# A decoder layer on one core: a wide stream in the first feed-forward product, GpSimd's squares moved into it, and a reordered opening

## What is computed

```
u = rms_norm(h, norm_mix);  z = u @ w_in                      # 1024 x 3328
h = h + concat(rwkv7_time_mix(z[:1792]), moba_attention(z[1792:])) @ w_mix_out
h = h + memory_cross_attention(rms_norm(h, norm_xattn), rms_norm(mem, norm_mem))   # w_xq, w_xkv, w_xo
a = square(relu(rms_norm(h, norm_ffn) @ w_ff1))               # 1024 x 4096
h = h + a @ w_ff2                                             # 4096 x 1024
out = rms_norm(h, norm_final)
```

## Time and profile before

| | us |
|---|---|
| median of 3 runs | 477.54 |
| lowest, highest | 476.89, 479.78 |
| the profiled execution | 479.23 |
| its span, first to last instruction | 477.2 |
| TensorE busy | 459.2 |
| VectorE busy | 316.0 |
| ScalarE busy | 235.7 |
| GpSimd busy | 34.8 |
| mean granted clock of TensorE | 0.994 |

### The profile page before, as it was taken

The page is one execution under the profiler, slowest core; times in us unless marked ns, Lnnn a source line. Parts: engine busy times, 40 slices in busy tenths (PEclk is TensorE's granted clock), DMA queues, the critical chain, the costliest instruction groups (busy, mean ns, idle before and its releaser), DMA issues.

```text
span 477.2 us, 11032 instructions
## 1 busy us (share of the span) xinstructions
PE 459.2 (96%) x4774; PEld 429.8 (90%) x4774; DVE 316.0 (66%) x459; ACT 235.7 (49%) x357; POOL 34.8 (7%) x50
## 2 busy tenths in 40 slices
PE   4999999999999999999999997999999999999994
PEld 4999999989898899999998997989898989898983
DVE  4688999897576459668656486555466555554646
ACT  5779843343354235335543453544374555453534
POOL 8100000000000000151000053000000000000000
PEclk9999999999999999999999998999999999999998
DMA  7963534505060523554452363756555555756602
GB/s 256 332 218 102 177 105 159 182 10 172 3 203 15 166 89 99 168 177 142 133 166 89 94 181 97 232 169 198 178 178 177 177 181 178 233 195 205 197 2 88
DMA packets 61411, 73.09 MB, mean 153 GB/s; under 512 B 1314, under 2 KB 51572, under 8 KB 61364
## 3 DMA queue, kind: packets, MB, share of 16 engines
q1 hardware_dynamic: 61284, 72.14, 47.3%
q0 software_dynamic: 80, 0.26, 0.1%
HBM read 71.35 MB, written 1.05 MB: 152 GB/s over the span
## 4 chain that ended last, share of the span: by engine, by line
PE 90%; DVE 5%; issue 1%; DMA 1%; ACT 1%; SPq 0%; ACTq 0%; DVEq 0%
PE bank L482 17%; PE bank L483 16%; PE bank L484 16%; PE bank L499 6%; PE bank L500 6%; PE bank L501 6%; PE bank L449 2%; PE bank L450 2%; PE bank L451 2%; PE bank L851 2%; DMA xval<-in_x 1%; PE bank L875 1%; PE bank L611 1%; DVE w_lo L1543 1%; PE bank L777 1%
## 5 line engine op out<-in xcount | busy, mean ns | idle before, releaser
L1543 DVE TENSOR_TENSOR w_lo<-raw,w_hi 128x1024 fp32r<-128x1024 f32 x130 | 160.3, 1242 | 84.2 <-ACT w_hi L1051 84.0
L1051 ACT ACTIVATE w_hi<-raw 128x1024 fp32r<-128x1024 f32 x130 | 136.6, 1057 | 140.0 <-PE bank L484 80.1
L482 PE MATMUL bank<-op_hi,w_hi 128*128 128x256 f32 x672 | 195.1, 290 | 3.8 <-DVE w_lo L1543 3.0
L483 PE MATMUL bank<-op_lo,w_hi 128*128 128x256 f32 x672 | 190.7, 284 | 0.4 <-issue 0.4
L484 PE MATMUL bank<-op_hi,w_lo 128*128 128x256 f32 x672 | 190.7, 284 | 0.0
L482 PEld LDWEIGHTS bank<-op_hi,w_hi 128*128 128x128 f32 x672 | 129.4, 192 | 6.7 <-issue 4.6
L483 PEld LDWEIGHTS bank<-op_lo,w_hi 128*128 128x128 f32 x672 | 129.5, 193 | 0.5
L484 PEld LDWEIGHTS bank<-op_hi,w_lo 128*128 128x128 f32 x672 | 129.4, 193 | 0.4 <-issue 0.4
L499 PE MATMUL bank<-w_hi,op_hi 128*128 128x512 f32 x128 | 49.9, 390 | 0.0
L500 PE MATMUL bank<-w_lo,op_hi 128*128 128x512 f32 x128 | 49.9, 390 | 0.0
L501 PE MATMUL bank<-w_hi,op_lo 128*128 128x512 f32 x128 | 49.8, 389 | 0.0
(11 more groups left out here) (247 smaller groups left out, 487.1 us busy)
## 6 DMA issues: line engine op xcount, KB each, us to landing
raw<-in_w_ff SPq DMA_DIRECT2D x32, 1024.0 KB, 5.4
raw<-in_w_in SPq DMA_DIRECT2D x12, 1024.0 KB, 5.5
raw<-in_w_xkv SPq DMA_DIRECT2D x8, 1024.0 KB, 5.7
raw<-in_w_mix_out SPq DMA_DIRECT2D x4, 1024.0 KB, 5.0
raw<-in_w_xq SPq DMA_DIRECT2D x4, 1024.0 KB, 5.1
raw<-in_w_xo SPq DMA_DIRECT2D x4, 1024.0 KB, 5.7
xval<-in_x SPq DMA_DIRECT2D x2, 512.0 KB, 4.8
raw<-in_w_in SPq DMA_DIRECT2D x2, 512.0 KB, 5.7
```

Of the source, the lines that this page charges most:

```text
L482: mm(dst, wh[:, k, :], op_hi[which][:, k, :], start=first, stop=False)
L483: mm(dst, wh[:, k, :], op_lo[which][:, k, :], start=False, stop=False)
L1051: op(view(w_hi), r, ACT.Copy).then_inc(hi_done, 1)
L1543: tt(view(w_lo), r, view(w_hi).bitcast(f32), ALU.subtract).then_inc(lo_done, 1)
```

## The change

- **Wide stream.** In `f1`, `op_hi[0]` and `op_lo[0]` become one tile `op_both[0]`, and for each k one matmul of 2 x 256 columns multiplies `w_hi` with both; one of 256 adds `w_lo` times `op_hi` to the left half of the bank. Each half has a bank of its own, in turn, and its result is the sum of the bank's two sides. ScalarE copies the right side out (`part`), VectorE adds the left (`add`) and does Relu and square in one (`square`), ScalarE rounds it to `op_hi[1]`, VectorE subtracts.
- **First f1 unit.** Its quarters run (66,0), (67,0), (66,1), (67,1), no longer with half 68 between.
- **GpSimd's squares** of `xo` wait besides for the ends of halves 67, 70, 73, 76; `rms(3)` moves from behind 27 quarters to behind 46.
- **Opening.** x comes in quarters; `norm_mix` is sent by ScalarE; unit 1 is sent ahead of the parameters; 14 identity products (`warm`) stand around the turns of x; VectorE's `copies(0)` moves behind `lo(3)`; some steps of the first six outputs are put in another order, `sums()` ahead of `take(3)` among them.

```diff
-    _late = {"mix": 0, "xo": 1, "f1": 1}.get(UNITS[_u][0])
+    _late = {"mix": 0, "xo": 1}.get(UNITS[_u][0])
...
-    elif _u == len(UNITS) - 1:
+    elif _u == len(UNITS) - 1 or UNITS[_u][0] == "f1" and UNITS[_u][4] == 0:
 
         QUARTERS += [(2 * _u + _i, _p) for _p in range(2) for _i in range(2)]
...
+        op_both = [sb("op0", [128, 2, KT, T], f32r), None]
+        op_hi = [op_both[0][:, 0, :, :], sb("op1_hi", [128, KT, T], f32r)]
+        op_lo = [op_both[0][:, 1, :, :], sb("op1_lo", [128, KT, T], f32r)]
...
+        def half_no(s):
+            return s - OUTS[FIRST["f1"]][1] if UNITS[s // 2][4] < 2 else 2 * UNITS[s // 2][4] + s % 2
+        def half_bank(s):
+            return dense_bank[(s + 1) % 2]
...
-            sp.dma_start(prow[0:8, :], io["norm_mix"].rearrange("l (r p) -> (l r) p", p=128)).then_inc(mix_in, 16)
...
             for half in range(2):
-                c, k = slice(512 * half, 512 * half + 512), slice(4 * half, 4 * half + 4)
-                sp.dma_start(stage[0][:, :, c], x[:, :, c]).then_inc(x_in[half], 16)
+                for q in (2 * half, 2 * half + 1):
+                    c = slice(256 * q, 256 * q + 256)
+                    sp.dma_start(stage[0][:, :, c], x[:, :, c]).then_inc(x_in[q], 16)
+                k = slice(4 * half, 4 * half + 4)
...
+            load_unit(1)
             for name, (r, c) in ROW.items():
...
-            load_unit(1)
...
                     pool.wait_ge(out_taken, FIRST[what] + j + 1)
+                    if count:
+                        pool.wait_ge(dense_mm, OUTS[FIRST["f1"]][1] + 2 + 3 * j)
...
+                    if what == "f1":
+                        half = half_no(s)
+                        if half < 2:
+                            pe.wait_ge(out_taken, FIRST["f1"] - 1 + half)
+                        else:
+                            pe.wait_ge(dve_add, half - 1)
...
+                if what == "f1":
+                    b = half_bank(s)
+                    for k in range(4 * part, 4 * part + 4):
+                        first, final = q == BEGUN[s] and k % 4 == 0, q == DONE[s] and k % 4 == 3
+                        if opening and k % 2 == 0:
+                            pe.wait_ge(dve_op, op_no("xo", k // 2) + 1)
+                        if final:
+                            mm(b[:, 0:T], wl[:, k, :], op_hi[0][:, k, :], start=False, stop=False)
+                        last = mm(b[:, :], wh[:, k, :], op_both[0][:, :, k, :], start=first, stop=final)
+                        if not final:
+                            mm(b[:, 0:T], wl[:, k, :], op_hi[0][:, k, :], start=False, stop=False)
...
+            def warm(n):
+                for _ in range(n):
+                    turn_op(dense_bank[1][:, 0:128], ident[:, :], ident[:, :])
...
             params(0)
+            warm(4)
             load(0, 0)
             load(0, 1)
+            warm(7)
             load(0, 2)
             load(0, 3)
+            warm(3)
+            dense(3)
+            params(1)
+            dense(1)
+            spread(0)
+            dense(9)
+            lora()
...
-            dense(27)
+            dense(46)
             rms(3)
-            dense(28)
+            dense(9)
             residual(0)
...
+            def part(n, half):
+                s = OUTS[FIRST["f1"] + n][1] + half
+                act.wait_ge(dense_mm, s + 1)
+                if n >= 2:
+                    act.wait_ge(dve_square, n - 1)
+                op(tmp[:, n % 2, T * half:T * half + T], half_bank(s)[:, T:2 * T], ACT.Copy).then_inc(act_part, 1)
             def hidden(o):
                 n = nth(o)
-                act.wait_ge(out_taken, o + 1)
+                act.wait_ge(dve_square, n + 1)
                 k = 4 * (n // 2 % 2) + 2 * (n % 2)
-                op(op_hi[1][:, k:k + 2, :], pair(tmp[:, n % 2, :]), ACT.Square).then_inc(act_hidden, 1)
+                op(op_hi[1][:, k:k + 2, :], pair(hid_sq[:, n % 2, :]), ACT.Copy).then_inc(act_hidden, 1)
...
+            def add(n, half):
+                s = OUTS[FIRST["f1"] + n][1] + half
+                dve.wait_ge(act_part, 2 * n + half + 1)
+                x = tmp[:, n % 2, T * half:T * half + T]
+                tt(x, half_bank(s)[:, 0:T], x, ALU.add).then_inc(dve_add, 1)
+            def square(n):
+                dve.wait_ge(dve_add, 2 * n + 2)
+                if n >= 2:
+                    dve.wait_ge(dve_hidden, n - 1)
+                x = tmp[:, n % 2, :]
+                stt(out=hid_sq[:, n % 2, :], in0=x, scalar=0.0, in1=x, op0=ALU.max, op1=ALU.mult).then_inc(dve_square, 1)
...
             params(0)
             load(0, 0)
-            copies(0)
+            lo(0)
             load(0, 1)
-            lo(0)
...
             spread_copy(0)
+            copies(0)
+            copies(1)
+            take(0)
             lo(4)
...
+            add(4, 0)
             lo(81)
+            add(4, 1)
+            square(4)
             lo(82)
+            hidden(4)
...
```

More of the change, by code:

```diff
@@ L1442, in _ @@
             hi(80)
+            part(4, 0)
             hi(81)
-            take(36)
+            part(4, 1)
             hi(82)
-            follow(36)
+            follow(37)
+            part(5, 0)
             hi(83)
+            part(5, 1)
             hi(84)
+            follow(38)
             hi(85)
-            take(37)
             hi(86)
@@ L1456, in _ @@
             hi(89)
-            follow(37)
-            take(38)
-            follow(38)
-            take(39)
+            part(6, 1)
+            hi(90)
             follow(39)
-            hi(90)
+            part(7, 0)
             hi(91)
-            take(40)
+            part(7, 1)
+            hi(92)
             follow(40)
-            hi(92)
             hi(93)
@@ L2151, in _ @@
             follow(32)
+            add(0, 0)
             lo(69)
-            follow(33)
+            add(0, 1)
+            square(0)
             lo(70)
+            hidden(0)
+            add(1, 0)
             lo(71)
+            add(1, 1)
+            square(1)
             lo(72)
+            hidden(1)
+            add(2, 0)
             lo(73)
+            add(2, 1)
+            square(2)
             lo(74)
-            follow(34)
+            hidden(2)
+            add(3, 0)
             lo(75)
+            add(3, 1)
+            square(3)
             lo(76)
-            follow(35)
+            hidden(3)
             lo(77)
@@ L2166, in _ @@
             lo(80)
+            add(4, 0)
             lo(81)
-            follow(36)
-            rms(3)
+            add(4, 1)
+            square(4)
             lo(82)
+            hidden(4)
+            add(5, 0)
             lo(83)
+            add(5, 1)
+            square(5)
             lo(84)
+            hidden(5)
             lo(85)
@@ L2175, in _ @@
             lo(87)
+            rms(3)
             lo(88)
+            add(6, 0)
             lo(89)
-            follow(37)
-            follow(38)
-            follow(39)
+            add(6, 1)
+            square(6)
             lo(90)
+            hidden(6)
+            add(7, 0)
             lo(91)
-            follow(40)
+            add(7, 1)
+            square(7)
             lo(92)
+            hidden(7)
             lo(93)
@@ L2188, in _ @@
             lo(96)
+            add(8, 0)
             lo(97)
-            follow(41)
+            add(8, 1)
+            square(8)
             lo(98)
+            hidden(8)
+            add(9, 0)
             lo(99)
-            follow(42)
+            add(9, 1)
+            square(9)
             lo(100)
+            hidden(9)
             lo(101)
@@ L2198, in _ @@
             lo(104)
+            add(10, 0)
             lo(105)
-            follow(43)
+            add(10, 1)
+            square(10)
             lo(106)
+            hidden(10)
+            add(11, 0)
             lo(107)
-            follow(44)
+            add(11, 1)
+            square(11)
             lo(108)
+            hidden(11)
             lo(109)
@@ L2208, in _ @@
             lo(112)
+            add(12, 0)
             lo(113)
-            follow(45)
+            add(12, 1)
+            square(12)
             lo(114)
+            hidden(12)
+            add(13, 0)
             lo(115)
-            follow(46)
+            add(13, 1)
+            square(13)
             lo(116)
+            hidden(13)
             lo(117)
@@ L2218, in _ @@
             lo(120)
+            add(14, 0)
             lo(121)
-            follow(47)
+            add(14, 1)
+            square(14)
             lo(122)
+            hidden(14)
+            add(15, 0)
             lo(123)
-            follow(48)
+            add(15, 1)
+            square(15)
             lo(124)
+            hidden(15)
             lo(125)
```

149 lines of the change are left out of this document (75 added, 74 removed).

## The result

| | before | after |
|---|---|---|
| median | 477.7 us (4 runs, 476.89 to 479.78) | 471.95 us (4 runs, 471.72 to 472.79) |
| the profiled execution | 479.23 | 472.15 |
| its span | 477.2 | 470.3 |
| TensorE busy | 459.2 | 457.3 |
| VectorE busy | 316.0 | 323.4 |

The ratio of the times is 0.9866, with a 95% interval of 0.984 to 0.9892: 1.3% faster (1.2% by the medians). The forecast was 469.8 in a range of 467.3 to 473.0. The medians lie 5.75 us apart, the profiled spans 6.9; the forecast had 7.9 and 9.3. So the kind of result is as forecast, and some 2 us of the gain are missing. The time lies in the range, but outside the stretch of 468.3 to 471 to which the forecast gave its 0.50.

The account below looks back on a forecast made before the run. TensorE, with 90% of the chain, was taken to bound the kernel. Seam 3.1, clock 1.5, wide stream 3.4, squares -0.2 and opening 1.5 made 9.3 us, giving 469.9 (469.7 without the dip); forecast 469.8, range 467.3 to 473.0.

Parts of the forecast that it names:

- The seam: Between xo and the first f1 product: TensorE's 3.2 us stall shrinks to some 0.1; gain 3.1 us.
- The clock's dip: Behind the stall at xo to f1: without that pause the granted clock should not fall to 0.50; gain 1.5 us.
- The wide stream: In f1: one 512-column matmul replaces two of 256, 0.360 us per k becomes 0.347; gain 3.4 us.
- The handshake: Rival in f1: late adds make every half wait 0.5 us, 16 us in all, giving 485.8; chance 0.04.
- The squares' new cover: In f1: GpSimd's held-back squares hold up VectorE there; 0.2 us put on the path, 1.5 if nothing overlaps.
- (a): Opening: only four turns and three identity products follow x's last quarter; first product at 9.7, 0.35 us sooner.
- (b): Opening: 14 identity products keep TensorE working nearly throughout, so the clock is up by the first product; worth 1.6 us.
- (c): Opening, a cap: unit 1 needs lo(2), whose chain moves only with x's last quarter; start 16.4, gain 1.5 us.
- (d): Opening: load_unit(1) passes the parameter loads, which come at about 12.5; TensorE asks at 14.0, covered by 1.5 us.
- (e): Opening: copies(0) moves behind lo(3), where VectorE's waits cover it; bare, it would cost 1.3 us.
- (f): Past 39 us: the opening's gain lives only if VectorE's whole string moves too, which it does.
- the opening gives nothing: Rival: VectorE's string from 39 to 84 us stays put and TensorE only waits longer there; 471.3 us, chance 0.14.

Follow-up runs that it names:

- Experiment 3: The changed kernel without GpSimd's wait for the f1 halves, so the xo squares start again as soon as hT is taken; 476.13 us (ratio 0.9954).
- experiment 4: The kernel before with only GpSimd's xo squares held back to the ends of halves 67, 70, 73, 76 and rms(3) moved; 475.4 us (ratio 0.9942).
- experiment 1: The changed kernel with op_hi and op_lo of one k laid out as 512 columns in a row; 472.34 us (ratio 0.9877).
- experiment 2: The changed kernel with the wide matmul taken apart into two of 256 columns; 474.42 us (ratio 0.9931).
- experiment 7: The changed kernel with x in two halves instead of four quarters; 472.04 us (ratio 0.9857).
- experiment 5: The changed kernel with each f1 quarter's four wide matmuls in a row and four narrow ones in a row; 472.55 us (ratio 0.987).
- experiment 8: The changed kernel with the whole opening of the kernel before, keeping the change's seam, squares and wide stream; 471.87 us (ratio 0.9861).

## Why the prediction was right, and where it was not

**The seam: right, 3.2 us for 3.1.** The walk put `follow(31)` at 0.87 and (67,0) at 285.8. The pair took 0.88, and the matmul starts at 285.75. Experiment 3 brings the stalls back by one edit, and experiment 4 shows the two halves of the cause apart.

**The clock's dip: right, 1.4 in the profile for 1.5.** The window is at 1.00. No run without the stall of 3.2 us shows the dip, not even experiments 3 and 4 with stalls of 1.4 to 1.9. Whether the timed executions of the kernel before have it was open. Beside experiments 1 to 4 its eight executions had mean clocks of 0.992 to 0.999: the three at 0.996 and above took 477.7 to 478.0 us, the five at 0.992 to 0.994 478.1 to 479.1. Beside the later ones 27 more had 0.992 to 0.999, with 6 at 0.996 and above; where both kinds ran on one chip, the groups' means lie 0.9 and 1.4 us apart. If that difference is the dip, most have it (26 of 35), and it is worth 0.8 to 1.4 us in the times. The profiled execution of the kernel before lies 1.5 above its median, which is why the spans differ by 1.1 us more than the medians do.

**The wide stream: the mechanism was right, the size was off.** The term was 256 x 0.0133 = 3.4; it measured 2.1 to 2.5. The step that failed is "both row forms carry the same 13 ns [...], so it belongs to the instruction". The rows it was taken from are runs of one shape. With shapes in turn the pair costs 5 ns more than the sum of both: the wide one 8 more, the narrow one 3 less. In rows the sum of the two pitches is 0.350, and 3 ns a pair stay. What they are is open: not the operand in two pieces (experiment 1), nor, by more than 2 ns, a busy VectorE (a wide one's mean is 0.236 where VectorE works for most of it and 0.234 elsewhere). The bound below, 0 to 0.6, was wrong too: experiment 2 excludes it.

**What it costs the others: right.** No half of `f1` waited for an `add`: TensorE's timeline has no wait over 0.15 us behind 264.81, with VectorE at 9.09 of 10 in the window from 290 to 300. The handshake, the rival on the other side, did not decide anywhere.

**The squares' new cover: 0.2 forecast, nothing seen.** The window 290 to 300 holds two of GpSimd's instructions and TensorE is busy for all of it. VectorE was held, as the forecast had it: its `square` at 291.73 takes 1.08 us instead of 0.69, its `lo` at 308.70 2.31 instead of 1.23. TensorE did not wait for it.

**The opening: wrong, about nothing for 1.5.** Three steps failed in the changed kernel's profile. In experiment 1's, with the same opening, the first product starts at 9.61 and the clock is up, as (a) and (b) had it; unit 1 still starts at 17.24 instead of 16.4, and 0.8 us reaches `xo` instead of 1.5. So what the forecast made of the cap, (c), fails in all five profiles with this opening (unit 1 at 17.24 to 18.59), (a) and (b) in four.
- (a), "Only four turns (0.8) and three identity products (0.6) follow the last quarter", from 8.3 on. The third quarter landed at 8.76 and the fourth at 9.52, when the third's turns were nearly done (9.71), so eight turns stand behind the wait (1.76 us), then three identity products (0.50). x came later, not sooner, since it came in quarters (experiment 7): 8.81 instead of 8.44 for the first matmul behind the wait, and complete at 9.52 instead of 8.39. Over the profiles with the new order of loads that start is at 8.15 to 9.24; with the old order at 7.93 to 8.56. So the first product starts at 11.07, which is the 8.81 + 1.76 + 0.50 of the rows.
- (b), "the clock should be up by the first product". It rose 0.55 us behind it, at 11.62, after a wait of 1.46 us for x in the middle of the identity products. That is 2.0 us sooner than before, which is worth half of that, and the first product is 1.0 later.
- (c), the cap: named rightly, placed wrongly. ScalarE, in the changed kernel's timeline:

```profile
8.05 1.06 ACT L1093 ACTIVATE w_hi<-raw 128x1024 fp32r<-128x1024 f32 x1 [2.29 <-DMA raw<-in_w_in]
9.01 2.64 ACT L1145 ACTIVATE op<-bank,par 128x256 fp32r<-128x256 f32 x6
11.54 1.06 ACT L1093 ACTIVATE w_hi<-raw 128x1024 fp32r<-128x1024 f32 x1
12.49 1.06 ACT L1158 ACTIVATE neu<-xval 128x1024 f32<-128x1024 f32 x1
```

`hi(0)` waits for the first half of unit 0's weights until 8.05 and holds up six operands behind it (before: `hi(0)` at 7.42, four operands behind x at 9.59). The sums of squares begin at 12.49; before they did at 12.12. So the split of halves 2 and 3 starts on VectorE at 16.52, later than 15.95 and not 0.8 sooner, and unit 1 can't start before about 17.7. The chain does not move "only with the last quarter". It also goes through the first weights, which landed at 8.03 instead of 6.21, and through TensorE, which turns the parameters (`params(1)`) behind three quarters in the new order and not behind two: VectorE waited 0.64 us for them in experiment 1 and 0.51 in experiment 7, where ScalarE's sums were as early as in the kernel before (12.14) and the split still starts at 16.58.
- (d), "covered by 1.5 us", held by luck. TensorE asked for the parameters at 15.7, not at 14.0, because its first product was late. In experiment 1, where that started at 9.61 and TensorE asked at 14.0, it waited 1.0 us. The loads had been summed as bytes; that SP would stand 2.1 to 3.8 us at the first of the parameters was left out.

(e) and (f) held: no wait for `copies(0)` shows, and a lead or a lag at 18 us was still there at 100. The rival "the opening gives nothing" had the right result with the wrong reason: it had VectorE's string stay put from 39 to 84 us.

In sum: the profile's 6.9 is 9.3 less 1.5 for the opening, 1.3 for the wide stream and 0.1 for the dip, and with 0.1 more than forecast in the seam, 0.2 for the squares, which cost nothing, and 0.2 unassigned. The time lies 2.15 us above the forecast. Two terms were too large together, a case that no rival had; the range held it because it reached to either alone, and that is luck in part.

## What to carry to other kernels

A pitch read from a run of one shape is a bound for a stream of mixed shapes, not its price: take a mixed row, or leave a third of the gain open. In an opening that waits for DMA, do not take it that a load cut into smaller ones lands sooner: here x in quarters was complete 0.3 us or more later than in any profile with halves. Follow the second engine's chain through every operand it waits for, and look at more than one profile, since the clock and the landings of the same opening differed by over a us. Hold a GpSimd instruction away from the stretch where VectorE's two-input instructions feed TensorE, and put it where VectorE's result is not due.

## What the runs showed of the hardware that was not expected

- In turn, a 512-column matmul is followed after 0.235 us and a 256-column one after 0.117; runs of one shape have 0.227 (`f2`) and 0.120. The slow ones are those with a 256-column one ahead (0.233 in experiment 5), not those with one behind (0.227). Eight wide ones in a row in `f1` have a mean of 0.230, with the first four of the row the slowest.
- A VectorE instruction with two inputs in SBUF that begins while a GpSimd instruction runs is held until that one is over (2.31 us instead of 1.23 at 308.70 in the changed kernel); one that had begun before it, or has an input in PSUM, is not.
- A clock that has risen can fall behind a short wait. In two of the seven profiles with the new opening or a variant of it that has identity products (experiments 3 and 5) it rose ahead of the wait for x and was at 0.50 for 3.4 us behind it (10.2 to 13.6 in experiment 3). Identity products ahead of a wait that they do not fill are a risk, and those behind it cost their time.
- SP stood 1.7 to 3.8 us at one DMA of 4 KB when 3 MB (x, unit 0 and unit 1) had been issued just ahead of it, and 0.4 to 0.7 us when it was 2 MB (x and unit 0).
- TensorE has now and then a wait of 0.2 to 0.6 us that the profile puts down to `issue`: at 84.25 in the kernel before, at 125.14 in the changed one (0.46; the 0.38 us by which it is ahead at 102 us are gone behind it), at neither place in experiment 8. It comes and goes between profiles, and makes a difference of half a us between two of them uncertain.
